# The last output tile of a hybrid decoder's down projection: own buffer for its third weight, an earlier first split, and its second half in two parts of 128 tokens

## The chip, the cores and the metric

The kernel runs on one core of one Trainium2 chip. Its time is the device time of one execution in microseconds (us), and lower is better. TensorE (PE in the profile) multiplies matrices out of SBUF into PSUM, ScalarE (ACT), VectorE (DVE) and GpSimd (POOL) work elementwise, and the queues of SyncE (SP) and POOL issue transfers.

## The reference, cut to what matters

One inference step of a decoder layer for 544 tokens (512 of a prompt, 32 of samples), model width 1024. Everything before the feed-forward network is left out here, since the change does not touch it:

```python
def rmsnorm(x, g):
    x32 = x.astype(jnp.float32)
    y = x32 * lax.rsqrt(jnp.mean(x32 * x32, axis=-1, keepdims=True) + RMS_EPS)
    return (y * g.astype(jnp.float32)).astype(x.dtype)
...
    f = rmsnorm(x, g_ffn_pre)
    g_, u_ = jnp.split(f @ w_gate_up, 2, axis=-1)
    x = x + rmsnorm((jax.nn.silu(g_) * u_) @ w_down, g_ffn_post)
```

`w_down` has 2816 rows (22 blocks of 128) and 1024 columns (8 tiles of 128). The change is in the last of the 8 tiles of `(silu(g) * u) @ w_down` and in the norm, the residual sum and the store that follow it.

## The kernel before, in words

**Products.** The output is made transposed, one tile of 128 output columns at a time: the weight block (128x128) is loaded into TensorE, the tokens stream through it, and the tile stands in PSUM as 128 columns by 544 tokens. To keep precision with the one-pass number format, each factor is split into a rounded high part and the rest: ScalarE writes `w_hi` by a copy (`hi`), VectorE writes `w_lo = w_raw - w_hi` (`lo`), and each block of 128 rows of `w_down` costs three matmuls per piece of tokens: high by high, low by high, high by low. Each of these matmuls loads its own 128x128 weights first, which the profile shows as LDWEIGHTS on a row of its own, PEld.

**Order of the end.** Tile 0 is made plainly, tiles 1 to 6 two at a time by a scheme with fewer products (`block_product`, `plain_rest`, L1571 and L1586), and tile 7, the last, plainly again by `down_steps` (L1533). Its weights come in three chunks of 8, 8 and 6 blocks, c = 0, 1, 2 (`DOWN_K`), in two ring slots: chunk 0 in slot 1, chunk 1 in slot 0, chunk 2 in slot 1 again. So chunk 2 can be transferred to `w_raw[1]` only after chunk 0 was split, and split only after chunk 0's products are done. On the SP queue its transfer also stands behind the 12 transfers of tile 5's `move_y`.

**Halves.** For the last tile the 544 tokens are cut at `LAST_CUT` = 288: half 0 is 256 prompt tokens and the 32 samples, half 1 the other 256 prompt tokens. Token rows are taken two apart, so token tiles `tt` = 0 and 1 are the even and the odd tokens of half 0, `tt` = 2 and 3 those of half 1, and `TT` = 4 are the samples. Chunk 0 is multiplied for both halves, then chunks 1 and 2 for half 0; then, while half 1's chunks 1 and 2 are multiplied, half 0 goes through its chain: ScalarE takes squares and scaled values out of PSUM (`y_half`), TensorE sums the squares over the 1024 columns by matmuls with a column of ones (`sum_part`: of `yacc`, the squares of tiles 0 to 6, and of `ysq`, those of tile 7) and transposes the tile (`half_T`), ScalarE takes the root (`y_roots`) and copies the transposed tile to `ytok` (`half_copy`), VectorE takes the reciprocal and makes `ytok * 1/rms + x1tok` for each token tile in one pass of 1024 columns (L2872), and SP stores it. When half 1's products are done, the same chain runs for half 1 with nothing beside it.

**Moves.** Tiles 0 to 6 reach `ytok` by a 32x32 block transpose on VectorE and 12 small transfers per tile (`move_y`): tiles 0 to 4 on POOL's queue, tiles 5 and 6 on SP's.

Of the kernel before, what the change touches and what calls it, by code (L numbers as in the profile page):

```python
# [130 lines left out]
def program(nc, x_prompt, x_sample, cache_k, cache_v, page_table, state_conv, state_h,  # L131
# [251 lines left out]
    with ExitStack() as ctx:  # L383
# [271 lines left out]
        def _(sp_):  # L655
# [269 lines left out]
        def _(e):  # L925
# [139 lines left out]
            e.dma_start(x1tok[:, 0, :], token_rows(x1_dram, 0)).then_inc(x1_back, 16)  # L1065
            e.dma_start(x1tok[0:TS, TT, :], x1_dram[SEQ:T, :]).then_inc(x1_back, 16)


        @block.tensor
        def _(e):  # L1070
# [545 lines left out]

            def sum_part(sums, tts):

                for tt in tts:
                    rows = TS if tt == TT else P  # L1620
                    mm = e.matmul(y_total(tt)[0:rows], y_cols(sums[:, :], tt), ones[:, 0:1],
                                  start=sums is yacc, stop=sums is ysq, skip_group_check=True)
                return mm

            def half_T(h):

                e.wait_ge(y_free, KD + 2 + h)
                e.wait_ge(yt_free, h + 1)
                for tt in (0, 1) if h == 0 else (2, 3):
                    mm = e.transpose(ps[:, YT_BANK, tt * P:tt * P + P], y_cols(yg[1][:, :], tt), ident[:, :])  # L1630
                if h == 0:
                    mm = e.transpose(ps[0:TS, YT_BANK + 1, 0:P], y_cols(yg[1][:, :], TT), ident[:, :])
                mm.then_inc(yt_ready, 1)
# [27 lines left out]
        def _(e):  # L1661
# [486 lines left out]
            def y_half(h):  # L2148

                m, cols = KD - 1, slice(LAST_CUT, T) if h else slice(0, LAST_CUT)  # L2150
                n = cols.stop - cols.start
# [3 lines left out]
                e.activation(ysq[:, cols], ps[:, D_PAIR_BANK + h, 0:n], ACT.Square).then_inc(y_sq_last, 1)  # L2155
                e.activation(yg[1][:, cols], ps[:, D_PAIR_BANK + h, 0:n], ACT.Identity, scale=prm[:, m + 48:m + 49]
                             ).then_inc(y_free, 1)

            def y_roots(h):

                e.wait_ge(yn_ready, h + 1)
                tts = slice(2 * h, 2 * h + 2)
                sums = ps[:, 2:4, 0] if h else ps[:, 2 * D_PAIR[0], tts]
                last = e.activation(ycol[:, tts], sums, ACT.Sqrt, bias=eps_col[:, :], scale=1.0 / D)
                if h == 0:
                    last = e.activation(ycol[0:TS, TT:TT + 1], y_total(TT)[0:TS], ACT.Sqrt, bias=eps_col[0:TS, :],
                                        scale=1.0 / D)
# [24 lines left out]
            for n in range(N7):  # L2192
# [36 lines left out]
        def _(e):  # L2229
# [605 lines left out]
            for n in range(N7):  # L2835
# [66 lines left out]
```

## Time and profile before

| | us |
|---|---|
| median of 3 runs | 765.9 |
| lowest and highest | 765.15 and 766.57 |
| the profiled execution's own time | 766.97 |
| its span, first to last instruction | 765.2 |

The span leaves out what lies around the first and the last instruction, so it is shorter than the execution's own time by 1.77 us. The profiled execution is 1.07 us slower than the median of the runs. Lines of the profile name the engine, the source line, the operation, and output<-input; a shape such as `128*128 128x256` is the loaded weight block and the streamed operand.

### The profile page before, as it was taken

To read this page: it belongs to the slowest core of one execution; us is meant where nothing else is said; L and a number is where in the kernel's file an instruction comes from. 1 tells how busy PE (TensorE), PEld (TensorE's weight loads), DVE (VectorE), ACT (ScalarE), POOL (GpSimd) and SP (SyncE) were. 2 spreads that over 40 slices of the span, in tenths; PEclk is the share of its full clock that TensorE was granted. 3 is DMA by queue.
4 is the path that set the end of the run, shared out by engine and by line. 5 is a ranking of instruction groups with operands and counts; after the bars stand their busy time and mean duration, and the time that the engine had idled before them with its cause. 6 is when DMAs were issued, how large, how long until landed. Compare 5 with 4: busy or idle time off the path is not lost.

```text
span 765.2 us, 16115 instructions
## 1 busy us (share of the span) xinstructions
PE 753.7 (98%) x5909; PEld 713.0 (93%) x5909; DVE 520.2 (68%) x822; ACT 376.4 (49%) x670; POOL 109.2 (14%) x216
## 2 busy tenths in 40 slices
PE   8999999999999999999999999999999999999995
PEld 6998899898898999987899999999999999999995
DVE  7547747656665575784569887787777899665543
ACT  7334725534733642343466555545545468444432
POOL 6602012020120110013000000000000000363510
PEclk9999999999999999999999999999999999999998
DMA  8645555545543315515561333323333212434283
GB/s 260 168 112 118 156 136 115 149 102 114 148 123 99 90 57 170 165 65 179 169 194 29 111 110 110 96 80 98 110 110 104 60 49 84 136 90 112 63 230 129
DMA packets 187065, 91.77 MB, mean 120 GB/s; under 512 B 54582, under 2 KB 179978, under 8 KB 187020
## 3 DMA queue, kind: packets, MB, share of 16 engines
q1 hardware_dynamic: 181342, 82.97, 39.6%
q0 software_dynamic: 4496, 7.85, 3.4%
q8 instruction: 28, 0.46, 0.3%
q10 hardware_dynamic: 1182, 0.35, 0.2%
q14 instruction: 17, 0.14, 0.1%
HBM read 82.37 MB, written 6.81 MB: 117 GB/s over the span
## 4 chain that ended last, share of the span: by engine, by line
PE 93%; DVE 2%; DMA 2%; SPq 1%; ACT 1%; issue 0%; DVEq 0%
PE ps L1080 34%; PE ps L1469 28%; PE ps L1363 6%; PE ps L1586 6%; PE ps L1571 5%; PE ps L1533 3%; PE ps L1437 3%; PE ps L1187 1%; PE ps L1201 1%; PE ps L1219 1%; DMA w_raw<-in_w_down_dram 1%; DMA w_raw<-in_w_in_dram 1%; SPq L647 1%; PE ps L1261 1%; PE ps L1172 1%; PE ps L1371 1%
## 5 line engine op out<-in xcount | busy, mean ns | idle before, releaser
L1080 PE MATMUL ps<-xin_hi,w_hi 128*128 128x272 f32 x544 | 117.1, 296 | 1.2 <-DVE w_lo L2256 1.2
L1080 PE MATMUL ps<-xin_hi,w_lo 128*128 128x272 f32 x544 | 112.5, 288 | 0.0
L1080 PE MATMUL ps<-xin_lo,w_hi 128*128 128x272 f32 x544 | 112.2, 288 | 0.0
L2249 DVE TENSOR_TENSOR w_lo<-w_raw,w_hi 128x1024 fp32r<-128x1024 f32 (+1 forms) x47 | 56.9, 1210 | 58.8 <-ACT w_hi L1666 58.4
L1080 PEld LDWEIGHTS ps<-xin_hi,w_hi 128*128 128x128 f32 x544 | 84.8, 188 | 9.5 <-issue 7.6
L1080 PEld LDWEIGHTS ps<-xin_lo,w_hi 128*128 128x128 f32 x544 | 85.4, 188 | 0.0
L1080 PEld LDWEIGHTS ps<-xin_hi,w_lo 128*128 128x128 f32 x544 | 85.0, 189 | 0.0
L1666 ACT ACTIVATE w_hi<-w_raw 128x1024 fp32r<-128x1024 f32 (+1 forms) x48 | 50.1, 1045 | 55.6 <-PE ps L1080 45.4
L647 POOL DMA_DIRECT2D ytok<-yz x40 | 28.1, 709 | 307.6 <-DVE yz L2810 307.6
L1469 PE MATMUL ps<-xq_lo,b_hi 128*128 128x272 f32 x160 | 46.6, 292 | 0.0
L1469 PE MATMUL ps<-xq_hi,a_lo 128*128 128x272 f32 x160 | 46.4, 290 | 0.0
L1469 PE MATMUL ps<-xq_lo,a_hi 128*128 128x272 f32 x160 | 46.2, 289 | 0.0
L1469 PE MATMUL ps<-xq_hi,b_hi 128*128 128x272 f32 x160 | 46.2, 288 | 0.0
L1469 PE MATMUL ps<-xq_hi,b_lo 128*128 128x272 f32 x160 | 46.1, 288 | 0.0
L1469 PE MATMUL ps<-xq_hi,c_hi 128*128 128x272 f32 x160 | 46.1, 288 | 0.0
L1469 PE MATMUL ps<-xq_hi,a_hi 128*128 128x272 f32 x160 | 46.1, 288 | 0.0
L1469 PE MATMUL ps<-xq_hi,c_lo 128*128 128x272 f32 x160 | 45.9, 287 | 0.0
L1469 PE MATMUL ps<-xq_lo,c_hi 128*128 128x272 f32 x160 | 45.9, 287 | 0.0
L1988 ACT ACTIVATE a_hi<-g_raw 128x1024 fp32r<-128x1024 f32 x20 | 21.2, 1062 | 20.8 <-PE ps L1469 17.9
L1469 PEld LDWEIGHTS ps<-xq_hi,b_hi 128*128 128x128 f32 x160 | 30.2, 188 | 0.0
L1469 PEld LDWEIGHTS ps<-xq_hi,b_lo 128*128 128x128 f32 x160 | 30.1, 188 | 0.0
L1469 PEld LDWEIGHTS ps<-xq_lo,a_hi 128*128 128x128 f32 x160 | 30.1, 188 | 0.0
(394 smaller groups left out, 2134.7 us busy)
## 6 DMA issues: line engine op xcount, KB each, us to landing
w_raw<-in_w_in_dram SPq DMA_DIRECT2D x68, 256.0 KB, 3.3
g_raw<-in_w_gate_up_dram SPq DMA_DIRECT2D x40, 256.0 KB, 3.8
u_raw<-in_w_gate_up_dram SPq DMA_DIRECT2D x20, 256.0 KB, 3.1
e_raw<-in_w_gate_up_dram SPq DMA_DIRECT2D x20, 256.0 KB, 4.3
raw_p<-in_w_down_dram SPq DMA_DIRECT2D x24, 192.0 KB, 2.6
kc<-in_cache_k_dram SPq DMA_DIRECT2D x64, 64.0 KB
vc<-in_cache_v_dram SPq DMA_DIRECT2D x64, 64.0 KB
raw<-in_w_down_dram SPq DMA_DIRECT2D x12, 320.0 KB, 3.1
```

The source lines that it names most:

```text
L647: e.dma_start(prompt[:, 2 * part:2 * part + 2, d, :], yz[s][rows, c0:c0 + 2 * P]).then_inc(moved, 16)
L1080: mm = e.matmul(ps[:, bank + h, 0:HT], wt[:, kw, :], xt[:, kx, h * HT:h * HT + HT], start=first and wt is wh and xt is xh, stop=last and ( ...
L1172: e.matmul(ps[GR * g:GR * g + GR, S_BANK, 0:PAST], q_bd[:, b, :], kcT[:, b, :], start=b < NG, stop=b >= NG, skip_group_check=True)
L1363: mm = e.matmul(ps[:, o_bank(tt) + c, :], xt[:, k, tt * P:tt * P + P], wt[:, c * NHALF:(c + 1) * NHALF], start=k == K_ORDER[0] and xt is x ...
L1437: mm = e.matmul(ps[:, 4 * m + 2 * c + h, 0:HT], wt[:, k, :], xt[:, x, k % KQ, :], start=k == 0 and wt is wh and xt is xq_hi, stop=k == KD ...
L1469: mm = e.matmul(ps[:, bank, 0:HT], wt[:, k0 + k, :], xt[:, x, k, :], start=first and k == 0 and wt is wh and xt is xq_hi, stop=last and k ...
L1533: mm = e.matmul(ps[:, D_BANK[odd] + h, 0:cols.stop - cols.start], wt[:, k, :], x, start=first and k == ks[0] and wt is wh and not lo_x, st ...
L1571: mm = e.matmul(ps[:, bank, 0:HT], wt[:, k, :], xt, start=first and k == 0 and wt is wh and xt is xh, stop=last and k == SK - 1 and wt is ...
L1586: mm = e.matmul(ps[:, banks[h], 0:HT], wt[:, k, :], x, start=firsts[h] and i == 0 and k == 0 and wt is wh and not lo_x, stop=lasts[h] and ...
L1666: e.activation((to or w_hi[s])[:, 0:k, :], w_raw[s][:, 0:k, :], ACT.Copy).then_inc(hi_done, count)
L1988: e.activation(a_hi[:, :, :], g_raw[s][:, :, :], ACT.Copy).then_inc(a_h, 1)
L2249: e.tensor_tensor(wl[:, 0:k, :], w_raw[s][:, 0:k, :], wh[:, 0:k, :].bitcast(F32), ALU.subtract).then_inc(lo_done, count)
```

## The change

What it does, by engine:

- A buffer `raw_last` for chunk 2's raw weights, in the place of `hs[0]`, which the pair scheme has finished reading by then. SP issues its transfer right after those of chunks 0 and 1, behind a wait on `op_used`, and tile 5's 12 transfers go to the end of POOL's queue.
- ScalarE's split of chunk 0 waits for one piece less of tile 5 and 6's products (`OPS7 * N7 - 2` for `- 1`); VectorE's half of it has the old wait.
- Half 1 is made in two parts of 128 tokens (`last_part`), the even and the odd tokens, each in its own PSUM bank, read from `hid_hi` and `hid_lo` with a stride of two. The end has three stages instead of two: half 0, part 0, part 1.
- VectorE adds half 0's squares of tile 7 to `yacc`, so half 0's sums need one matmul for each token tile instead of two.

The diff, cut to its core:

```diff
+    raw_last = put("raw_last", [P, DOWN_K[2], P], where=[hs_at[0]])
...
-            for part in range(3):
-                move_y(e, KD - 3, 1, part, y_moved_last)
-            load(C_LAST + 2, 1, wd[:, KF - DOWN_K[2]:KF, (KD - 1) * P:KD * P], DOWN_K[2])
+            e.wait_ge(op_used, OP_0 + OPS7 * (N7 - 1) + OP_S1 + 1)
+            e.dma_start(raw_last[:, :, :], wd[:, KF - DOWN_K[2]:KF, (KD - 1) * P:KD * P]).then_inc(raw_in["11"], 16)
...
+            def last_part(c, ks, part, last):
+
+                wh, wl = w_hi[(1 + c) % 2], w_lo[(1 + c) % 2]
+                k0 = sum(DOWN_K[:c])
+                out = ps[:, LAST_BANK[part], 0:P]
+                for k in ks:
+                    for wt, lo_x in ((wh, False), (wh, True), (wl, False)):
+                        x = (hid_lo[:, k0 + k, LAST_CUT:T] if lo_x else hid_hi[k0 + k][:, LAST_CUT:T]
+                             ).rearrange("p (n s) -> p s n", s=2)
+                        mm = e.matmul(out, wt[:, k, :], x[:, part], start=c == 0 and k == 0 and wt is wh and not lo_x,
+                                      stop=last and k == ks[-1] and wt is wl, skip_group_check=True)
+                return mm
...
-            down_steps(0, 1, range(DOWN_K[0]), True, False, cut=LAST_CUT).then_inc(tile_done, 1)
+            down_steps(0, 1, range(DOWN_K[0]), True, False, hs=(0,), cut=LAST_CUT)
+            last_part(0, range(DOWN_K[0]), 0, False)
+            last_part(0, range(DOWN_K[0]), 1, False).then_inc(tile_done, 1)
             for c in (1, 2):
                 split_ready(last + c)
                 mm = down_steps(c, 1, range(DOWN_K[c]), False, c == 2, hs=(0,), cut=LAST_CUT)
             mm.then_inc(tile_done, 1)
-            down_steps(1, 1, range(4), False, False, hs=(1,), cut=LAST_CUT)
-            e.wait_ge(ysq_used, KD)
-            for tt in (0, 1, TT):
-                sum_part(yacc, (tt,))
-                if tt == 0:
-                    e.wait_ge(y_sq_last, 1)
-                mm = sum_part(ysq, (tt,))
-            mm.then_inc(yn_ready, 1)
+            last_part(1, range(6), 0, False)
+            e.wait_ge(ysq_used, KD + 1)
+            sum_part(yacc, (0, 1, TT), True).then_inc(yn_ready, 1)
             half_T(0)
-            down_steps(1, 1, range(4, DOWN_K[1]), False, False, hs=(1,), cut=LAST_CUT)
-            down_steps(2, 1, range(DOWN_K[2]), False, True, hs=(1,), cut=LAST_CUT).then_inc(tile_done, 1)
-            sum_part(yacc, (2, 3))
+            last_part(1, range(6, DOWN_K[1]), 0, False)
+            last_part(2, range(DOWN_K[2]), 0, False).then_inc(tile_done, 1)
+            last_part(1, range(DOWN_K[1]), 1, False)
+            sum_part(yacc, (2,))
             e.wait_ge(y_sq_last, 2)
-            sum_part(ysq, (2, 3)).then_inc(yn_ready, 1)
+            sum_part(ysq, (2,)).then_inc(yn_ready, 1)
             half_T(1)
+            last_part(2, range(DOWN_K[2]), 1, True).then_inc(tile_done, 1)
+            sum_part(yacc, (3,))
+            e.wait_ge(y_sq_last, 3)
+            sum_part(ysq, (3,)).then_inc(yn_ready, 1)
+            half_T(2)
...
-            e.wait_ge(op_used, OP_0 + OPS7 * N7 - 1)
+            e.wait_ge(op_used, OP_0 + OPS7 * N7 - 2)
             hi(C_LAST, C_LAST // 2, 1, DOWN_K[0])
...
+            e.wait_ge(op_used, OP_0 + OPS7 * N7 - 1)
             lo(C_LAST, 1, DOWN_K[0])
```

The first place is the end of SP's queue, from the transfers of chunks 0 and 1 (`w_raw_50`, `w_raw_49`) to tile 6's `move_y`. Before:

```order
L668 DMA w_raw_50<-in_w_down_dram 128x4x128 [waits lo_done,s_done]
L668 DMA w_raw_50<-in_w_down_dram 128x4x128
L668 DMA w_raw_49<-in_w_down_dram 128x4x128 [waits lo_done]
L668 DMA w_raw_49<-in_w_down_dram 128x4x128
L647 DMA ytok<-yz_216 128x2x32 [waits y_turned,consts]
L647 DMA ytok<-yz_216 128x2x32 x7
L649 DMA ytok<-yz_216 32x32 x4
L668 DMA w_raw_50<-in_w_down_dram 128x4x128 [waits lo_done]
L668 DMA w_raw_50<-in_w_down_dram 128x2x128
L647 DMA ytok<-yz_215 128x2x32 [waits y_turned,consts]
L647 DMA ytok<-yz_215 128x2x32 x7
L649 DMA ytok<-yz_215 32x32 x4
```

After:

```order
L670 DMA w_raw_50<-in_w_down_dram 128x4x128 [waits lo_done,s_done]
L670 DMA w_raw_50<-in_w_down_dram 128x4x128
L670 DMA w_raw_49<-in_w_down_dram 128x4x128 [waits lo_done]
L670 DMA w_raw_49<-in_w_down_dram 128x4x128
L909 DMA raw_last<-in_w_down_dram 128x6x128 [waits s_mm]
L649 DMA ytok<-yz_215 128x2x32 [waits y_turned,consts]
L649 DMA ytok<-yz_215 128x2x32 x7
L651 DMA ytok<-yz_215 32x32 x4
```

Chunk 2's transfer now stands ahead of all of `move_y`, and tile 5's 12 transfers (`yz_216`) have left this queue; tile 6's (`yz_215`) stay.

The second place is TensorE where half 0's sums and transposes stand between the products of the other half (`w_hi_51` and `w_lo_53` are chunk 1's split weights, `w_hi_52` and `w_lo_54` chunk 2's). Before:

```order
L1533 MATMUL ps<-hid_hi_203,w_hi_51 128x256 [waits hid_l]
L1533 MATMUL ps<-hid_lo,w_hi_51 128x256
L1533 MATMUL ps<-hid_hi_203,w_lo_53 128x256
L1621 MATMUL ps<-ones,yacc 128x1 [waits ysq_used]
L1621 MATMUL ps<-ones,ysq 128x1 [waits y_sq_last]
L1621 MATMUL ps<-ones,yacc 128x1
L1621 MATMUL ps<-ones,ysq 128x1
L1621 MATMUL ps<-ones,yacc 32x1
L1621 MATMUL ps<-ones,ysq 32x1
L1630 MATMUL ps<-ident,yg_227 128x128 [waits yt_free,y_free]
L1630 MATMUL ps<-ident,yg_227 128x128
L1632 MATMUL ps<-ident,yg_227 32x128
```

After:

```order
L1629 MATMUL ps<-hid_lo,w_hi_51 128x128
L1629 MATMUL ps<-hid_hi_205,w_lo_53 128x128
L1638 MATMUL ps<-ones,yacc 128x1 [waits ysq_used]
L1638 MATMUL ps<-ones,yacc 128x1
L1638 MATMUL ps<-ones,yacc 32x1
L1647 MATMUL ps<-ident,yg_227 128x128 [waits yt_free,y_free]
L1647 MATMUL ps<-ident,yg_227 128x128
L1652 MATMUL ps<-ident,yg_227 32x128
L1629 MATMUL ps<-hid_hi_206,w_hi_51 128x128
```

The three sums of `ysq` are gone, and the products around them are 128 columns wide instead of 256. In the last tile as a whole there were 66 matmuls of 128x256 and there are 132 of 128x128; the 66 of 128x288 are unchanged.

The third place is the end of VectorE's program. Before:

```order
L2249 TENSOR_TENSOR w_lo_54<-w_raw_50,w_hi_52 128x768 [waits hi_done]
L2862 RECIPROCAL ycol<-ycol 128x2 [waits y_root,x1_back]
L2864 RECIPROCAL ycol<-ycol 32x1
L2872 SCALAR_TENSOR_TENSOR ytok<-ytok,ycol,x1tok 128x1024 [waits y_moved,y_moved_last,yt_free,y_inv]
L2872 SCALAR_TENSOR_TENSOR ytok<-ytok,ycol,x1tok 128x1024
L2872 SCALAR_TENSOR_TENSOR ytok<-ytok,ycol,x1tok 32x1024
L2862 RECIPROCAL ycol<-ycol 128x2 [waits y_root]
L2872 SCALAR_TENSOR_TENSOR ytok<-ytok,ycol,x1tok 128x1024 [waits y_moved,y_moved_last,yt_free,y_inv]
L2872 SCALAR_TENSOR_TENSOR ytok<-ytok,ycol,x1tok 128x1024
```

After:

```order
L2885 TENSOR_TENSOR w_lo_54<-raw_last,w_hi_52 128x768 [waits hi_done]
L2890 TENSOR_TENSOR yacc<-yacc,ysq 128x288 [waits ysq_used,y_sq_last]
L2895 RECIPROCAL ycol<-ycol 128x2 [waits y_root,x1_back]
L2897 RECIPROCAL ycol<-ycol 32x1
L2905 SCALAR_TENSOR_TENSOR ytok<-ytok,ycol,x1tok 128x1024 [waits y_moved,y_moved_last,yt_free,y_inv]
L2905 SCALAR_TENSOR_TENSOR ytok<-ytok,ycol,x1tok 128x1024
L2905 SCALAR_TENSOR_TENSOR ytok<-ytok,ycol,x1tok 32x1024
L2895 RECIPROCAL ycol<-ycol 128x1 [waits y_root]
L2905 SCALAR_TENSOR_TENSOR ytok<-ytok,ycol,x1tok 128x1024 [waits y_moved,y_moved_last,yt_free,y_inv]
L2895 RECIPROCAL ycol<-ycol 128x1 [waits y_root]
L2905 SCALAR_TENSOR_TENSOR ytok<-ytok,ycol,x1tok 128x1024 [waits y_moved,y_moved_last,yt_free,y_inv]
```

The addition to `yacc` is new, and the last group of two passes over `ytok` has become two groups of one.

## Rows read from the trace of the kernel before

**Rows 1.** The page, busy time: us, share of the span, instructions.

```profile
PE 753.7 (98%) x5909; PEld 713.0 (93%) x5909; DVE 520.2 (68%) x822; ACT 376.4 (49%) x670; POOL 109.2 (14%) x216
```

**Rows 2.** Windows, 748 to 757 us.

```profile
748.00:757.00 9.00, 8.69 (x72) 8.65 (x73) 2.81 (x5) 2.50 (x8) 0.00 (x0) 1.00 0.16 29
```

**Rows 3.** Timeline of TensorE: start us, us, engine, line, what, count.

```profile
736.71 0.41 PE L1586 MATMUL ps<-hid_hi,op_lo 128*128 128x272 f32 x2
...
737.28 0.52 PE L1533 MATMUL ps<-hid_hi,w_hi 128*128 128x288 f32 x2
...
737.63 0.41 PE L1533 MATMUL ps<-hid_lo,w_hi 128*128 128x288 f32 x2
...
743.40 0.29 PE L1533 MATMUL ps<-hid_hi,w_hi 128*128 128x288 f32 x1
...
746.46 0.29 PE L1533 MATMUL ps<-hid_hi,w_lo 128*128 128x288 f32 x1
...
748.31 0.40 PE L1533 MATMUL ps<-hid_hi,w_hi 128*128 128x288 f32 x1 [1.55 <-DVE w_lo L2249]
...
748.55 0.30 PE L1533 MATMUL ps<-hid_lo,w_hi 128*128 128x288 f32 x1
...
752.22 0.29 PE L1621 MATMUL ps<-ones,yacc 128*128 128x1 f32 x2
...
753.94 0.28 PE L1533 MATMUL ps<-hid_lo,w_hi 128*128 128x256 f32 x1
...
757.24 0.28 PE L1533 MATMUL ps<-hid_hi,w_lo 128*128 128x256 f32 x1
...
757.36 0.52 PE L1621 MATMUL ps<-ones,yacc 128*128 128x1 f32 x4
```

**Rows 4.** Timeline of ScalarE, VectorE, SP and POOL, 714 to 755 us.

```profile
714.40 5.62 POOL L647 DMA_DIRECT2D ytok<-yz  x8 [3.90 <-DVE yz L2810]
...
728.16 3.17 SPq L668 DMA_DIRECT2D w_raw<-in_w_down_dram  x4
...
734.90 1.06 ACT L1666 ACTIVATE w_hi<-w_raw 128x1024 fp32r<-128x1024 f32 x1 [2.57 <-PE ps L1586]
...
736.00 1.23 DVE L2249 TENSOR_TENSOR w_lo<-w_raw,w_hi 128x1024 fp32r<-128x1024 f32 x1 [1.81 <-ACT w_hi L1666]
...
742.58 1.13 SPq L668 DMA_DIRECT2D w_raw<-in_w_down_dram  x2
...
746.42 0.84 ACT L1666 ACTIVATE w_hi<-w_raw 128x768 fp32r<-128x768 f32 x1 [6.20 <-DMA w_raw<-in_w_down_dram]
...
747.29 0.96 DVE L2249 TENSOR_TENSOR w_lo<-w_raw,w_hi 128x768 fp32r<-128x768 f32 x1 [5.69 <-ACT w_hi L1666]
...
754.65 3.67 DVE L2872 SCALAR_TENSOR_TENSOR ytok<-ytok,ycol,x1tok 128x1024 f32<-128x1024 f32 x3 [0.47 <-ACT ytok L2177]
```

**Rows 5.** Timeline of TensorE's weight loads at two places.

```profile
748.31 0.19 PEld L1533 LDWEIGHTS ps<-hid_hi,w_hi 128*128 128x128 f32 x1 [1.79 <-DVE w_lo L2249]
...
748.42 0.19 PEld L1533 LDWEIGHTS ps<-hid_lo,w_hi 128*128 128x128 f32 x1
...
757.24 0.55 PEld L1621 LDWEIGHTS ps<-ones,yacc 128*128 128x128 f32 x4
```

**Rows 6.** Groups of weight loads by form, then one timeline row of TensorE.

```profile
L1533 PEld LDWEIGHTS ps<-hid_hi,w_hi 128*128 128x128 f32 x88 | 14.6, 188 | 2.3 <-DVE w_lo L2249 2.2
...
L1201 PEld LDWEIGHTS ps<-ident,lgt 128*128 128x128 f32 x80 | 9.0, 141 | 2.6 <-issue 2.5
...
7.64 0.38 PE L1125 MATMUL ps<-bktab,rel 128*128 128x128 f32 x2
```

**Rows 7.** Timeline of ScalarE, VectorE and SP after the last product.

```profile
757.56 0.38 ACT L2155 ACTIVATE ysq<-ps 128x256 f32<-128x256 f32 x1 [3.01 <-PE ps L1533]
...
759.46 2.48 DVE L2872 SCALAR_TENSOR_TENSOR ytok<-ytok,ycol,x1tok 128x1024 f32<-128x1024 f32 x2 [0.33 <-ACT ytok L2174]
...
760.77 1.53 SPq L915 DMA_DIRECT2D out_dram<-ytok  x2
```

More of the change, by code:

```diff
@@ L633, in program @@
         D_PAIR_BANK = 2 * D_PAIR[1]
+        LAST_BANK = (2 * D_PAIR[1] + 1, 2 * D_PAIR[0] + 1)
         def move_y(e, m, s, part, moved):
@@ L1066, in _ @@
             e.dma_start(x1tok[0:TS, TT, :], x1_dram[SEQ:T, :]).then_inc(x1_back, 16)
+            for part in range(3):
+                move_y(e, KD - 3, 1, part, y_moved)
         @block.tensor
@@ L1615, in _, with sum_part @@
                 plain_rest(n, OP_P2, (C21_BANK, C22_BANK), (False, False), (True, True))
-            def sum_part(sums, tts):
+            def last_part(c, ks, part, last):
[9 more added lines that the diff above has]
+                return mm
+            def sum_part(sums, tts, whole=False):
                 for tt in tts:
                     rows = TS if tt == TT else P
-                    mm = e.matmul(y_total(tt)[0:rows], y_cols(sums[:, :], tt), ones[:, 0:1],
-                                  start=sums is yacc, stop=sums is ysq, skip_group_check=True)
+                    x = sums[:, LAST_CUT + (tt - 2) * P:LAST_CUT + (tt - 1) * P] if sums is ysq else y_cols(sums[:, :], tt)
+                    mm = e.matmul(y_total(tt)[0:rows], x, ones[:, 0:1],
+                                  start=sums is yacc, stop=sums is ysq or whole, skip_group_check=True)
                 return mm
@@ L1628, in half_T @@
                 e.wait_ge(yt_free, h + 1)
-                for tt in (0, 1) if h == 0 else (2, 3):
+                for tt in (0, 1) if h == 0 else ():
                     mm = e.transpose(ps[:, YT_BANK, tt * P:tt * P + P], y_cols(yg[1][:, :], tt), ident[:, :])
+                if h > 0:
+                    c0 = LAST_CUT + (h - 1) * P
+                    mm = e.transpose(ps[:, YT_BANK, (h + 1) * P:(h + 2) * P], yg[1][:, c0:c0 + P], ident[:, :])
                 if h == 0:
@@ L2148, in y_half @@
             def y_half(h):
-                m, cols = KD - 1, slice(LAST_CUT, T) if h else slice(0, LAST_CUT)
-                n = cols.stop - cols.start
+                m = KD - 1
+                c0, n = (LAST_CUT + (h - 1) * P, P) if h else (0, LAST_CUT)
+                cols = slice(c0, c0 + n)
+                got = ps[:, LAST_BANK[h - 1], 0:P] if h else ps[:, D_PAIR_BANK, 0:n]
                 e.wait_ge(tile_done, C_LAST + 4 + h)
@@ L2154, in y_half @@
                     e.wait_ge(ysq_used, m + 1)
-                e.activation(ysq[:, cols], ps[:, D_PAIR_BANK + h, 0:n], ACT.Square).then_inc(y_sq_last, 1)
-                e.activation(yg[1][:, cols], ps[:, D_PAIR_BANK + h, 0:n], ACT.Identity, scale=prm[:, m + 48:m + 49]
+                e.activation(ysq[:, cols], got, ACT.Square).then_inc(y_sq_last, 1)
+                e.activation(yg[1][:, cols], got, ACT.Identity, scale=prm[:, m + 48:m + 49]
                              ).then_inc(y_free, 1)
@@ L2161, in y_roots @@
                 e.wait_ge(yn_ready, h + 1)
-                tts = slice(2 * h, 2 * h + 2)
-                sums = ps[:, 2:4, 0] if h else ps[:, 2 * D_PAIR[0], tts]
+                tts = slice(h + 1, h + 2) if h else slice(0, 2)
+                sums = y_total(h + 1) if h else ps[:, 2 * D_PAIR[0], tts]
                 last = e.activation(ycol[:, tts], sums, ACT.Sqrt, bias=eps_col[:, :], scale=1.0 / D)
@@ L2170, in half_copy @@
             def half_copy(h):
-                m, tts = KD - 1, slice(2 * h, 2 * h + 2)
+                m, tts = KD - 1, slice(h + 1, h + 2) if h else slice(0, 2)
                 e.wait_ge(yt_ready, h + 1)
                 last = e.activation(ytok[:, tts, m * P:m * P + P],
-                                    ps[:, 4, 2 * h * P:2 * h * P + 2 * P].rearrange("p (tt c) -> p tt c", c=P), ACT.Copy)
+                                    ps[:, 4, tts.start * P:tts.stop * P].rearrange("p (tt c) -> p tt c", c=P), ACT.Copy)
                 if h == 0:
@@ L2219, in _ @@
             y_pair(KD - 2, 0, c_pair[1], 5 * N7)
-            hi(C_LAST + 2, (C_LAST + 2) // 2, 1, DOWN_K[2])
+            e.wait_ge(raw_in["11"], raw_0["11"] + 16 * N7 + 16)
+            e.wait_ge(tile_done, C_LAST + 3)
+            e.activation(w_hi[1][:, 0:DOWN_K[2], :], raw_last[:, :, :], ACT.Copy).then_inc(hi_done, 1)
             e.activation(ycol[:, 15:16], eps_col[:, :], ACT.Sqrt)
-            for h in range(2):
+            for h in range(3):
                 y_half(h)
@@ L2855, in _ @@
             y_square(KD - 2, 0)
-            lo(C_LAST + 2, 1, DOWN_K[2])
+            e.wait_ge(hi_done, C_LAST + 3)
+            e.tensor_tensor(w_lo[1][:, 0:DOWN_K[2], :], raw_last[:, :, :], w_hi[1][:, 0:DOWN_K[2], :].bitcast(F32), ALU.subtract
+                            ).then_inc(lo_done, 1)
+            e.wait_ge(y_sq_last, 1)
+            e.wait_ge(ysq_used, KD)
+            e.tensor_tensor(yacc[:, 0:LAST_CUT], yacc[:, 0:LAST_CUT], ysq[:, 0:LAST_CUT], ALU.add).then_inc(ysq_used, 1)
             e.wait_ge(x1_back, 16 * (TT + 1))
-            for h in range(2):
-                tts = slice(2 * h, 2 * h + 2)
+            for h in range(3):
+                tts = slice(h + 1, h + 2) if h else slice(0, 2)
                 e.wait_ge(y_root, h + 1)
-                last = e.reciprocal(ycol[:, 8 + 2 * h:10 + 2 * h], ycol[:, tts])
+                last = e.reciprocal(ycol[:, 8 + tts.start:8 + tts.stop], ycol[:, tts])
                 if h == 0:
@@ L2867, in _ @@
                 e.wait_ge(yt_free, h + 2)
-                e.wait_ge(y_moved, 192 * (KD - 3))
-                e.wait_ge(y_moved_last, 2 * 192)
-                for tt in (0, 1, TT) if h == 0 else (2, 3):
+                e.wait_ge(y_moved, 192 * (KD - 2))
+                e.wait_ge(y_moved_last, 192)
+                for tt in (0, 1, TT) if h == 0 else (h + 1,):
                     rows = slice(0, P if tt < TT else TS)
```

## The prediction

> **What bounds the kernel now.** The page's busy times come first: TensorE is busy 98% of the span, no other engine more than 68% [rows 1], so only two things can move the time: TensorE's own work, and the places where it waits or where work follows its last product. The granted clock is 1.00, the 2.4 GHz level, in the stretch of the change [rows 2], so the clock is not one of them. Next the timeline of TensorE over the last tile [rows 3], read for the distance from one start to the next, since a matmul's duration of 0.28 to 0.30 overlaps its neighbours. A matmul of 288 columns comes every 0.133 us (743.40 to 746.46 in 23 steps), one of 256 every 0.118 us (753.94 to 757.24 in 28 steps). Two breaks stand out. After 736.71, a pair 0.25 apart should have been followed at 736.96, but the last tile starts at 737.28, and its first pair takes 0.35 instead of 0.25: 0.42 us lost. After 746.46 the next was due at 746.59 and came at 748.31, and its first step is 0.24 instead of 0.13: 1.83 us lost. The timelines of the other engines tell why [rows 4]: for the first, ScalarE's split starts at 734.90, released by TensorE, and VectorE's at 736.00, 1.23 long. For the second, chunk 2's transfer is issued only at 742.58, ScalarE splits it at 746.42 after 6.20 us of waiting for it, and VectorE at 747.29. Last, what follows the last product at 757.24 with nothing beside it [rows 3, 7]: sums, squares and a copy, then two passes of VectorE in 2.48 us from 759.46, and the second store after that.
>
> **The change, term by term.** The sum is made on the profiled execution's span, 765.2, at the slot after the last product, 757.36 [rows 3], and then for what follows it.
>
> *First split, -0.42.* ScalarE's wait is shortened by one piece, 9 pairs at 0.25, so it may start 2.25 us before 734.90, at 732.65. Its data is issued from 728.16 on [rows 4]. Chunk 2 took 3.84 us from its issue at 742.58 to ScalarE's start; the same lag from the second transfer, some 0.5 later than 728.16, gives 732.5. So ScalarE ends its 1.06 by about 734, VectorE, which keeps the old wait, starts at 734.9 and ends at 736.15, ahead of 736.96. The loss goes as a whole. Were the cover gone it would cost those 0.42 again.
>
> *Third weight, -1.83.* Chunk 2's transfer follows chunk 1's at about 731.3 (728.16 + 3.17) and lands, by the same 3.84 us, near 735.2, or a little later behind its neighbours. What is late next is the wait for chunk 0's products, since the split still goes into slot 1. With the widths below, chunk 0 ends at 736.96 + 24 x 0.133 + 48 x 0.112 = 745.5, the split needs the 1.89 us that it took from ScalarE's start to TensorE's (746.42 to 748.31), so it is ready at 747.6, and TensorE gets there at 745.5 + 24 x 0.133 = 748.7. Hidden, with 1.1 us to spare.
>
> *Moved transfers, 0.* Tile 5's 12 transfers leave SP, where they stood between 731.3 and 742.6, for POOL, which takes 5.62 us for 8 such [rows 4] and less for the four small ones. Even if they start 5 us later than on SP they are all issued by 750, and VectorE first reads `ytok` at 754.65 [rows 4]. POOL has nothing behind them. SP's tile 6 waits for VectorE's transpose as before.
>
> *The narrow parts, +7.0.* 66 matmuls of 256 columns, 66 x 0.118 = 7.8 us, become 132 of 128. The trace has no matmul of rounded factors under 256 columns, so this price is bounded. By columns alone it is 0.118 - 128 x 0.47 ns (the slope from 256 to 288) = 0.058 us. But each matmul brings its own weights, and a load has its own price. Two loads of rounded weights that find TensorE idle start 0.11 apart (748.31, 748.42), and four loads for matmuls of a single column, where nothing is to be streamed, take 0.55 us together, 0.118 apart [rows 5]. A load takes 188 ns in a record; the shorter loads of transposes, 141 ns, [rows 6] are another form and don't count here. At 256 columns stream and load are just equal, at 128 the load is longer. I take 0.112: nearer to 0.11, because `w_hi` and `w_lo` are read contiguously while the tiles under the 0.118 are read with the stride, and a little over it for the strided tokens, whose stream at 0.058 could double before it showed. 132 x 0.112 = 14.8, less 7.8.
>
> The row shows loads of 128 columns 0.11 us apart [rows 5]. The Trainium skill, "TensorE: Matmul & The Clock Gate", section "LDWEIGHTS (loading the stationary operand)", puts a load at its columns / 1.2 in ns, 107 for 128, which agrees and by which this term would be 6.3. The same page's section "Back-to-back issue gap" gives 81 ns as the sustained distance at 128 columns, by which it would be 2.9.
>
> *Half 0's sums, -0.5.* Of six instructions (12 records, from 752.22 on) three remain: four records at 0.118 and two short ones less. VectorE's new addition of 288 columns stands beside 18 products and is done before them.
>
> *Part 0's sums and transpose inside the stream, +0.7.* Four records of sums, 0.47, and one transpose with its change of form stand between products now; before, all of half 1's came behind the last.
>
> Sum up to the last product: -0.42 - 1.83 + 7.0 - 0.5 + 0.7 = +4.95, so the slot is at 762.3.
>
> *Behind it, -1.7.* One pass of VectorE instead of two: the second of 2.48 us goes, 1.20 [rows 7]. Two fewer records of sums, 0.24. Squares of 128 columns instead of 256 (0.38), 0.1; the copy, of the same size, 0.13 (both estimates, from a third of such a row's time going with its columns). Part 0's own pass starts near 760.7 and is over before part 1's, near 763.9. The last store follows the last pass by as much as before.
>
> Net 4.95 - 1.7 = **+3.25 us**: span 768.45, own time 770.2. That execution was 1.07 slower than the median, so on the median it is 765.9 + 3.25 = **769.2**.
>
> **The rivals.** What a measurement of this kernel can tell from no change is about 0.2%, 1.5 us.
>
> *The load hides and the columns decide (faster).* If the load of a narrow matmul went on beside the stream of the one before without limiting it, the distance would be 0.058 and the term -0.1 instead of +7.0: 765.9 - 3.9 = 762.0, with all the waits still hidden (chunk 0 would end at 743.0, the split be ready at 745.1, TensorE there at 746.2). It decides from 0.087 downwards, where the sum is zero. For it: loads are drawn as overlapping, and the busy row calls them so. Against it: the single-column matmuls, 0.118 apart with nothing else to wait for [rows 5]. 5%. A distance between, 0.08 to 0.1, gives 765 to 767.6; 3%. The 81 ns of the Trainium skill, "TensorE: Matmul & The Clock Gate", section "Back-to-back issue gap", would lead there, to 765.0, and no row of this trace bears it out.
>
> *Narrow rounded matmuls go at the raw price.* A raw matmul of 128 columns is two records in 0.38 us [rows 6], 0.11 apart, so 0.22 each. 132 of them cost 29, the term is 21 and the time 783. For it: nothing narrower than 256 occurs among the rounded ones, so no row excludes it. Against it: nothing in the rows shows a rounded matmul split in two at any width. 7%.
>
> *The strided read is slower than twice the contiguous one.* Then the distance is 0.125 to 0.15 and each 0.01 costs 1.3 us: 771 to 774. For it, the strided loads are 8 ns longer per record, a small sign; 5%.
>
> *A wait stays.* If chunk 2's split or tile 5's transfers came late, up to 1.83 would not be gained, 769.5 to 771. It changes only the size and is in the likeliest case's range.
>
> **How the numbers follow.** Forecast 80%: its own range is from 0.109 (-0.4) to 0.118 (+0.8) for the distance, 0.4 for the tail and the waits and as much for the median, 768.2 to 771.2. Together with half a us below, the wait that stays, and most of the strided case it gives 767.6 to 773, which leaves out the faster case, the one between and the raw price, 15%, and some edges. Slower by over 0.2%: 80 + 7 + 5 = 92%. Within 0.2%: 3%. Faster: 5%.
>
> **What would show it.** In the timeline after, the matmuls of 128x128 are 0.11 to 0.118 apart, and PEld fills that stretch without gaps; at 0.06 or 0.22 the step on the narrow parts is wrong. The breaks ahead of the last tile and of chunk 2 are gone, chunk 0's mark comes near 745.5, and the transfer of `raw_last` lands before 740. The last product stands near 762, followed by one pass of VectorE. If VectorE's first pass waited for a transfer, the step on moved transfers would be wrong. If the distance is right and the time still falls, a term that I don't see is in the end of the kernel.

## The result, and the profile after

| | before | after |
|---|---|---|
| median (lowest to highest), us | 766.13 (765.15 to 766.57), 6 runs | 769.17 (768.96 to 770.26), 6 runs |
| the profiled execution's own time, us | 766.97 | 768.96 |
| its span, us | 765.2 | 767.1 |

The change makes the kernel slower: the ratio of after to before is 1.0044, with a 95% interval of 1.0031 to 1.0057, which is 2.4 to 4.4 us. 769.2 had been forecast. Of all executions of this document two lie far from the rest, at a granted clock of 0.65 and 0.56 over their span (one of before, 1043.97 us, and one of the experiment that reads half 1 as two strided runs, 1223.14 us), and no ratio uses them.

The page of after, busy times as in [rows 1]: 60 instructions more on TensorE and 6.0 us more of its time.

```profile
PE 759.7 (99%) x5969; PEld 719.8 (94%) x5969; DVE 519.7 (68%) x824; ACT 376.6 (49%) x674; POOL 117.1 (15%) x228
```

The timeline of TensorE after, the places that answer to [rows 3] (start us, us, engine, line, what, count):

```profile
735.15 0.41 PE L1589 MATMUL ps<-hid_hi,op_lo 128*128 128x272 f32 x2
735.40 0.30 PE L1536 MATMUL ps<-hid_hi,w_hi 128*128 128x288 f32 x1
...
744.05 0.29 PE L1629 MATMUL ps<-hid_hi,w_lo 128*128 128x128 f32 x1
744.16 0.31 PE L1536 MATMUL ps<-hid_hi,w_hi 128*128 128x288 f32 x1
...
751.89 0.71 PE L1638 MATMUL ps<-ones,yacc 128*128 128x1 f32 x6
752.53 0.51 PE L1647 MATMUL ps<-ident,yg 128*128 128x128 f32 x2
...
753.07 0.31 PE L1629 MATMUL ps<-hid_lo,w_hi 128*128 128x128 f32 x1
...
758.43 0.32 PE L1629 MATMUL ps<-hid_hi,w_lo 128*128 128x128 f32 x1
758.57 0.31 PE L1638 MATMUL ps<-ones,yacc 128*128 128x1 f32 x2
...
759.03 0.36 PE L1629 MATMUL ps<-hid_hi,w_hi 128*128 128x128 f32 x1
...
761.05 0.32 PE L1629 MATMUL ps<-hid_hi,w_lo 128*128 128x128 f32 x1
```

Both breaks of [rows 3] are gone: the last tile starts at 735.40, 0.25 after the pair ahead of it, and no row up to 751.89 stands more than 0.16 behind its neighbour. The matmuls of 128 columns are 0.1165 apart (753.07 to 758.43 in 46 steps). Weight loads fill the whole last tile, 25.61 of 25.65 us, as the window from its first product to its last shows (stretch, its length, then busy us and instructions of PE, PEld, DVE, ACT and POOL, then the granted clock):

```profile
735.40:761.05 25.65, 25.65 (x214) 25.61 (x212) 10.11 (x14) 8.10 (x19) 6.88 (x11) 1.00 0.50 138
```

The timelines of the other engines after, which answer to [rows 4] and [rows 7]:

```profile
726.61 3.26 SPq L670 DMA_DIRECT2D w_raw<-in_w_down_dram  x4
729.90 0.51 SPq L909 DMA_DIRECT2D raw_last<-in_w_down_dram  x1
...
734.62 5.64 POOL L649 DMA_DIRECT2D ytok<-yz  x8
740.26 2.02 POOL L651 DMA_DIRECT2D ytok<-yz  x4
...
744.44 0.85 ACT L2247 ACTIVATE w_hi<-raw_last 128x768 fp32r<-128x768 f32 x1 [5.79 <-PE ps L1629]
745.32 0.96 DVE L2885 TENSOR_TENSOR w_lo<-raw_last,w_hi 128x768 fp32r<-128x768 f32 x1 [5.28 <-ACT w_hi L2247]
...
753.82 3.67 DVE L2905 SCALAR_TENSOR_TENSOR ytok<-ytok,ycol,x1tok 128x1024 f32<-128x1024 f32 x3 [0.47 <-ACT ytok L2202]
759.67 1.28 DVE L2905 SCALAR_TENSOR_TENSOR ytok<-ytok,ycol,x1tok 128x1024 f32<-128x1024 f32 x1
...
762.73 1.28 DVE L2905 SCALAR_TENSOR_TENSOR ytok<-ytok,ycol,x1tok 128x1024 f32<-128x1024 f32 x1
```

ScalarE's split of chunk 2 is now released by TensorE and no longer by a transfer: `raw_last`, issued at 729.90, landed 4.8 us later, at 734.7. One pass of VectorE, not two, follows the last product.

To compare executions, two lengths serve below. The *stage* runs from the start of the last pair product to the start of the last product of the last tile, the *tail* from there to the end of the span. Each execution reaches the stage at a moment of its own, though the kernels do the same in their first 700 us: this profiled run of before at 736.84, after at 735.28, and of the ten experiments nine at 735.4 to 736.2 and one at 737.3. The difference between before and after stands already at TensorE's 500th matmul, which starts at 67.69 in before and at 66.20 in after. That is why the spans differ by 2.0 us and the two lengths by 3.5. Each ratio compares a kernel with the runs of before that were made beside it, so the medians of the table do not all come from one set of runs.

| kernel | stage, us | tail, us | median, us | ratio to before (interval) |
|---|---|---|---|---|
| before | 20.40 | 7.94 | 766.13 | |
| after | 25.77 | 6.10 | 769.17 | 1.0044 (1.0031 to 1.0057) |
| third weight alone | 18.56 | 7.95 | 764.13 | 0.9971 (0.9959 to 0.9983) |
| earlier split alone | 20.23 | 7.93 | 766.96 | 1.0016 (1.0002 to 1.0030) |
| everything but the narrow parts | 17.61 | 7.95 | 763.33 | 0.9968 (0.9957 to 0.9980) |
| parts read contiguously | 25.12 | 6.06 | 768.67 | 1.0035 (1.0022 to 1.0047) |

### The profile page after: what moved, and what is told of

Same layout as the page of the kernel before. It is cut to its first block, busy times and chain, and to the rows that moved or that the text cites. A ratio compares the mean times of both kernels' runs of the same rounds, so it can differ in the third digit from the quotient of the medians.

```text
span 767.1 us, 16245 instructions
## 1 busy us (share of the span) xinstructions
PE 759.7 (99%) x5969; PEld 719.8 (94%) x5969; DVE 519.7 (68%) x824; ACT 376.6 (49%) x674; POOL 117.1 (15%) x228
## 4 chain that ended last, share of the span: by engine, by line
PE 97%; ACT 1%; DVE 1%; DMA 1%; issue 0%; ACTq 0%; DVEq 0%
PE ps L1083 34%; PE ps L1472 28%; PE ps L1589 7%; PE ps L1366 6%; PE ps L1574 5%; PE ps L1536 3%; PE ps L1440 3%; PE ps L1629 2%; PE ps L1190 1%; PE ps L1204 1%; PE ps L1222 1%; PE ps L1289 1%; PE ps L1264 1%; DMA rel<-in_rel_bias_dram 1%; PE ps L1374 1%; PE ps L1175 1%
## 5 line engine op out<-in xcount | busy, mean ns | idle before, releaser
L649 POOL DMA_DIRECT2D ytok<-yz x48 | 33.8, 711 | 307.4 <-DVE yz L2837 307.4
```

Source lines behind the costliest of these rows:

```text
L649: e.dma_start(prompt[:, 2 * part:2 * part + 2, d, :], yz[s][rows, c0:c0 + 2 * P]).then_inc(moved, 16)
```

## The experiments

### The parts of the change, one at a time

**Third weight alone.** Before, with `raw_last`, its transfer behind those of chunks 0 and 1, and tile 5's transfers on POOL.

```diff
-            load(C_LAST + 2, 1, wd[:, KF - DOWN_K[2]:KF, (KD - 1) * P:KD * P], DOWN_K[2])
+            e.wait_ge(op_used, OP_0 + OPS7 * (N7 - 1) + OP_S1 + 1)
+            e.dma_start(raw_last[:, :, :], wd[:, KF - DOWN_K[2]:KF, (KD - 1) * P:KD * P]).then_inc(raw_in["11"], 16)
```

> The kernel before with the own place for the third weight alone (its transfer early, tile 5's moves on POOL); widths, halves and the first split's wait as before. If the term for the third weight is right, the break of 1.83 us ahead of chunk 2 is gone and the time is 766.1 - 1.8 = 764.3. If the moves on POOL come late for VectorE's first pass, or the transfer collides with others, part of it comes back as a wait: 764.5 to 766. If the wait was not on the path that ended last, 766.1.

Measured: 764.13, ratio 0.9971. The stage is 1.84 us shorter, where the term was 1.83. The break ahead of chunk 2 is gone, the one ahead of the last tile stays, as the timeline of this kernel shows (in it the next pair would be due at 735.58):

```profile
735.33 0.41 PE L1588 MATMUL ps<-hid_hi,op_lo 128*128 128x272 f32 x2
735.89 0.40 PE L1535 MATMUL ps<-hid_hi,w_hi 128*128 128x288 f32 x1
...
746.39 0.30 PE L1535 MATMUL ps<-hid_hi,w_hi 128*128 128x288 f32 x1
746.52 0.30 PE L1535 MATMUL ps<-hid_lo,w_hi 128*128 128x288 f32 x1
```

**Earlier split alone.** Before, with the shorter wait of ScalarE.

```diff
-            e.wait_ge(op_used, OP_0 + OPS7 * N7 - 1)
+            e.wait_ge(op_used, OP_0 + OPS7 * N7 - 2)
             hi(C_LAST, C_LAST // 2, 1, DOWN_K[0])
...
+            e.wait_ge(op_used, OP_0 + OPS7 * N7 - 1)
             lo(C_LAST, 1, DOWN_K[0])
```

> The kernel before with the earlier first split alone. My theory: the 0.42 us between the pair scheme and the last tile goes, 765.7, which timing alone can't tell from 766.1; the timeline must show the last tile 0.25 us behind the last pair. Rival: ScalarE's new wait is replaced by the one for the transfer, and the gap stays above 0.3 us.

Measured: 766.96, ratio 1.0016 (1.0002 to 1.0030). The runs, 765.27 to 770.66, are thus 1.2 us slower than before, where the stage of the profiled one is 0.17 shorter and its tail the same; nothing in the end of the kernel shows this, and its cause is open. The timeline of TensorE has the first pair on time, but the break ahead of chunk 2 is longer, 2.09 from start to start instead of 1.85:

```profile
735.37 0.41 PE L1586 MATMUL ps<-hid_hi,op_lo 128*128 128x272 f32 x2
735.62 0.41 PE L1533 MATMUL ps<-hid_hi,w_hi 128*128 128x288 f32 x2
...
744.69 0.29 PE L1533 MATMUL ps<-hid_hi,w_lo 128*128 128x288 f32 x1
746.78 0.40 PE L1533 MATMUL ps<-hid_hi,w_hi 128*128 128x288 f32 x1 [1.79 <-DVE w_lo L2249]
```

TensorE reaches the wait for chunk 2 sooner, but that chunk's transfer still stands behind tile 5's twelve: it is issued 5.83 us after the start of the stage for 5.74 before, and ScalarE's split starts 9.39 after it for 9.58. So the stage falls by 0.17 of the 0.42. The edit is worth its term only together with the third weight.

**Everything but the narrow parts.** Both of these, VectorE's addition to `yacc`, and half 1 at 256 columns in two stages as before.

```diff
             down_steps(1, 1, range(4), False, False, hs=(1,), cut=LAST_CUT)
+            e.wait_ge(ysq_used, KD + 1)
+            sum_part(yacc, (0, 1, TT), True).then_inc(yn_ready, 1)
             half_T(0)
             down_steps(1, 1, range(4, DOWN_K[1]), False, False, hs=(1,), cut=LAST_CUT)
             down_steps(2, 1, range(DOWN_K[2]), False, True, hs=(1,), cut=LAST_CUT).then_inc(tile_done, 1)
```

> The changed kernel without the parts: own place for the third weight, earlier first split, half 0's squares added on VectorE, but half 1 as matmuls of 256 columns and the end in two stages as before. My sum: -0.42 - 1.83 - 0.5 = -2.75, so 763.4, and against the changed kernel -5.8. Rival (the parts cost less than I say and a wait takes their place): within 1 us of the changed kernel's 769.2. A second rival: the three gains overlap and give 764 to 765.

Measured: 763.33, ratio 0.9968, faster than both kernels. The stage is 2.79 us shorter than before's, where the three terms give 2.75; the 256-wide matmuls are 0.118 apart, as before (749.71 to 753.00 in 28 steps):

```profile
749.71 0.28 PE L1535 MATMUL ps<-hid_lo,w_hi 128*128 128x256 f32 x1
...
753.00 0.28 PE L1535 MATMUL ps<-hid_hi,w_lo 128*128 128x256 f32 x1
```

From here to after only the narrow parts are added: the stage grows by 8.16 and the tail falls by 1.85. So they alone cost 6.3 us by these marks, and (1.0044 - 0.9968) x 766 = 5.8 by the ratios.

### What a narrow matmul costs

**Parts read contiguously.** After, with the first and the last 128 tokens of half 1 as its parts.

```diff
-                        x = (hid_lo[:, k0 + k, LAST_CUT:T] if lo_x else hid_hi[k0 + k][:, LAST_CUT:T]
-                             ).rearrange("p (n s) -> p s n", s=2)
+                        c0 = LAST_CUT + P * part
+                        x = hid_lo[:, k0 + k, c0:c0 + P] if lo_x else hid_hi[k0 + k][:, c0:c0 + P]
```

> The changed kernel with part 0 and part 1 read as the first and the last 128 tokens of the half, without the stride of two; the last 128 output columns of these tokens come out in another order. If the weight load sets the distance, it stays at 0.116 to 0.118 us and the time at 769.2. If the strided read set it, the distance falls to 0.11 (768.3) or, if the columns alone would then decide, to 0.06 (761.5).

Measured: 768.67, stage 25.12, that is 0.65 less than after's. The distance is 0.1117 (753.64 to 757.66 in 36 steps) for 0.1165, and 132 x 0.0048 = 0.63. So the distance fell as it should have if the strided read had set it, but by 4.8 ns and no further, to what the weight loads alone take: the load sets the floor, and the stride adds a little above it. The ratios of the two kernels, 1.0035 and 1.0044, overlap in their intervals; what tells them apart is the trace.

```profile
753.64 0.28 PE L1629 MATMUL ps<-hid_lo,w_hi 128*128 128x128 f32 x1
...
757.66 0.28 PE L1629 MATMUL ps<-hid_lo,w_hi 128*128 128x128 f32 x1
```

**192 columns.** After, each narrow matmul with 192 contiguous columns.

```diff
-                out = ps[:, LAST_BANK[part], 0:P]
+                out = ps[:, LAST_BANK[part], 0:192]
...
+                        c0 = LAST_CUT + 64 * part
+                        x = hid_lo[:, k0 + k, c0:c0 + 192] if lo_x else hid_hi[k0 + k][:, c0:c0 + 192]
```

> The changed kernel with each of the 132 narrow matmuls widened to 192 contiguous columns (the two parts overlap, so the last tile's columns hold other tokens). By the slope of 0.47 ns per column, 192 columns alone would take 0.088 us. Load theory: still below the load's 0.111, so the distance is 0.111 and the time about 768.7. Stream theory (columns and load add up in part): 64 columns more cost up to 0.03 each, distance 0.115 to 0.14, time 769.3 to 772.6.

Measured: 769.38, ratio 1.0045 (1.0029 to 1.0062), stage 25.15. By the time alone this would be the stream theory (769.3 to 772.6), but stage and distance are those of 128 contiguous columns, so the 0.7 us between the two medians do not come from the matmuls. The distance is 0.1117 (753.51 to 757.64 in 37 steps):

```profile
753.51 0.28 PE L1629 MATMUL ps<-hid_hi,w_hi 128*128 128x192 f32 x1
...
757.64 0.28 PE L1629 MATMUL ps<-hid_lo,w_hi 128*128 128x192 f32 x1
```

A distance that does not change with the columns could also be a fixed price of every matmul, whatever it loads. The trace of before settles this: among half 0's sums the samples' matmuls load 32 columns of weights instead of 128, and these loads come 0.03 apart where those of 128 columns come 0.118 apart [rows 5]:

```profile
753.14 0.14 PEld L1621 LDWEIGHTS ps<-ones,yacc 128*32 128x32 f32 x2
753.20 0.14 PEld L1621 LDWEIGHTS ps<-ones,ysq 128*32 128x32 f32 x2
```

Their matmuls, of a single column like the others, start 0.03 to 0.05 apart. So the floor belongs to the 128x128 load.

**64 columns.** After, each narrow matmul with 64 contiguous columns.

```diff
-                out = ps[:, LAST_BANK[part], 0:P]
+                out = ps[:, LAST_BANK[part], 0:64]
...
+                        c0 = LAST_CUT + P * part
+                        x = hid_lo[:, k0 + k, c0:c0 + 64] if lo_x else hid_hi[k0 + k][:, c0:c0 + 64]
```

> The changed kernel with each of the 132 narrow matmuls cut to 64 contiguous columns; it leaves out half of half 1's tokens in the last output tile. Theory that the weight load sets the distance: 0.111 us as with 128 contiguous columns, the stage from the last pair product to the last product stays at 25.1 us, time about 768.7. Theory that the stream sets it, or a share of it: the distance falls towards 0.03 to 0.09, and the time by 132 times the difference, 758 to 766.5.

Measured: 777.09, ratio 1.0149 (1.0131 to 1.0168), which neither theory gave. The distance is what the load theory says, 0.1117 (740.91 to 745.38 in 40 steps), but then it doubles, between two matmuls of one kind with nothing waited for:

```profile
740.91 0.28 PE L1629 MATMUL ps<-hid_hi,w_hi 128*128 128x64 f32 x1
...
745.38 0.31 PE L1629 MATMUL ps<-hid_lo,w_hi 128*128 128x64 f32 x1
745.50 0.40 PE L1629 MATMUL ps<-hid_hi,w_lo 128*128 128x64 f32 x1
745.72 0.40 PE L1629 MATMUL ps<-hid_hi,w_hi 128*128 128x64 f32 x1
...
746.74 0.44 PE L1536 MATMUL ps<-hid_lo,w_hi 128*128 128x288 f32 x1
```

Windows of the same kernel (columns as above):

```profile
738.00:745.00 7.00, 7.00 (x62) 7.00 (x60) 3.02 (x5) 2.72 (x6) 6.33 (x11) 1.00 1.02 265
745.50:748.50 3.00, 3.00 (x15) 3.00 (x15) 0.96 (x1) 1.84 (x2) 0.00 (x0) 0.50 0.42 52
749.00:758.00 9.00, 9.00 (x77) 8.96 (x75) 1.57 (x4) 1.73 (x6) 0.00 (x0) 1.00 0.01 2
759.30:768.00 8.70, 8.70 (x43) 8.70 (x43) 2.90 (x4) 0.83 (x4) 0.00 (x0) 0.50 0.41 154
```

The granted clock falls from 1.00 to 0.50, the 1.2 GHz level, at 745.5, after 4.8 us of nothing but 64-column matmuls, comes back under the 288-wide ones of chunks 1 and 2 by 749, and is down again in the last stretch. At that level the 64-column matmuls are 0.213 apart. TensorE is shown busy all the time in all four stretches. With 128 columns at nearly the same distance it stays at 1.00, in after and in the contiguous version. The Trainium skill, "TensorE: Matmul & The Clock Gate", section "HAM oscillation — how this bites in real kernels", ties such a fall to gaps in which TensorE is idle; the rows above have none, so here the fall goes with the narrow stream alone. What in that stream brings it about is not shown.

**Stride of four.** After, with 64 columns read with a stride of four.

```diff
-                             ).rearrange("p (n s) -> p s n", s=2)
+                             ).rearrange("p (n s) -> p s n", s=4)
```

> The changed kernel with each of the 132 narrow matmuls reading 64 columns with a stride of four, over the same 256 columns as before; half of half 1's tokens are left out in the last output tile. If the 4.8 ns that the stride of two cost belong to each strided column, half the columns bring half of it, 0.1135 to 0.114, time about 768.4. If they belong to the reading of the whole 256 columns' memory, the distance stays at 0.116 or more, time about 769. If a strided read costs nothing once the stream is far shorter than the load, 0.111, time about 768.1.

Measured: 779.48, ratio 1.0169 (1.0151 to 1.0187), the clock again. At full clock the distance is 0.112 (739.44 to 741.67 in 20 steps), no more than with 64 contiguous columns. A strided stream of 64 columns shows nothing beside the load, so what a strided column costs had to be read where the stream is the longer one.

```profile
739.44 0.28 PE L1629 MATMUL ps<-hid_hi,w_lo 128*128 128x64 f32 x1
...
741.67 0.28 PE L1629 MATMUL ps<-hid_lo,w_hi 128*128 128x64 f32 x1
741.78 0.33 PE L1629 MATMUL ps<-hid_hi,w_lo 128*128 128x64 f32 x1
741.93 0.40 PE L1629 MATMUL ps<-hid_hi,w_hi 128*128 128x64 f32 x1
```

### What the stride costs

**256 columns, strided.** Two kernels on top of the version with two wide stages. The first reads half 1 as two strided runs of 128 columns in one matmul, the second as one strided run of 256 columns out of the first 512 tokens.

```diff
+                                x = x.rearrange("p (n s) -> p s n", s=2)
```

```diff
+                                x = (hid_lo[:, k0 + k, 0:512] if lo_x else hid_hi[k0 + k][:, 0:512]
+                                     ).rearrange("p (n s) -> p s n", s=2)[:, 0]
```

> The version of two 256-wide stages with the third weight's own place and the earlier split, in which half 1's 66 matmuls of 256 columns read their tokens with the stride of two, the even ones and then the odd ones (the last output tile's columns hold the tokens in another order). If the stride costs each column 0.0375 ns, as 4.8 ns over 128 would have it: 0.1175 becomes 0.127, the stage 17.6 becomes 18.2, time 763.3 becomes 763.9. If the 4.8 ns fall on each matmul whatever its width: 0.122, +0.3 us. If the stride costs only where the load is the longer one: 0.1175, no change.

> The version of two 256-wide stages, its half 1 reading every second one of the first 512 tokens as one strided run of 256 columns (so the last output tile's columns hold other tokens there). The version that read 256 tokens in two strided runs had a distance of 0.2285 us where the contiguous one has 0.1175. If the stride halves the rate of the stream, this one has 0.2285 too, stage 24.9 from the last pair product to the last product, time about 770.6. If the two runs cost it (each at least about 0.114), one run has 0.1175, stage 17.6, time 763.3.

Measured: 770.65, ratio 1.0054 (1.0034 to 1.0075), stage 24.86 for the first; 770.24, ratio 1.0051 (1.0037 to 1.0065), stage 24.87 for the second. None of the three prices that I had set for the first was near: its distance is 0.229 (756.66 to 760.78 in 18 steps), twice the contiguous one:

```profile
756.66 0.43 PE L1539 MATMUL ps<-hid_hi,w_lo 128*128 128x256 f32 x1
...
760.78 0.43 PE L1539 MATMUL ps<-hid_hi,w_lo 128*128 128x256 f32 x1
```

The second shows that the stride does it, and not the two runs (756.59 to 760.48 in 17 steps of 0.229):

```profile
756.59 0.43 PE L1538 MATMUL ps<-hid_hi,w_hi 128*128 128x256 f32 x1
...
760.48 0.42 PE L1538 MATMUL ps<-hid_hi,w_lo 128*128 128x256 f32 x1
```

**256 columns in two contiguous runs.**

```diff
+                                x = (hid_lo[:, k0 + k, 0:512] if lo_x else hid_hi[k0 + k][:, 0:512]
+                                     ).rearrange("p (s n) -> p s n", s=2)[:, :, 0:P]
```

> The same version, its half 1 reading two contiguous runs of 128 tokens each (0 to 127 and 256 to 383, so the last output tile's columns hold other tokens there) in one matmul of 256 columns. If the stride halves the rate, there is none here: distance 0.1175, stage 17.6, time 763.3. If two runs in one operand cost it, 0.2285, stage 24.9, time 770.6. If both, between.

Measured: 763.17, ratio 0.9958 (0.9943 to 0.9973), stage 17.70: two runs cost nothing that the stage shows, the distance is 0.118 (750.28 to 753.58 in 28 steps).

```profile
750.28 0.28 PE L1540 MATMUL ps<-hid_lo,w_hi 128*128 128x256 f32 x1
...
753.58 0.28 PE L1540 MATMUL ps<-hid_hi,w_lo 128*128 128x256 f32 x1
```

So a stride of two halves the rate of the stream: 0.229 / 256 = 0.89 ns per column for 0.46. A narrow strided matmul streams for 128 x 0.89 = 0.114, just past the load's 0.111 to 0.112. That is where some 3 of the 4.8 ns of the changed kernel come from; the other 2 are not explained. The Trainium skill, "SBUF — State Buffer", section "Specifications (TRN2)", asks for at least two hits in each 16-byte line for full bandwidth, and says that each step to a new line has a penalty, without its size. A stride of two over 4-byte elements has two hits in a line, and here it runs at half the rate (0.229 for 0.118 us): by the first half of that rule it would not, and the measurement decides.

## Why the prediction was right

**First split, -0.42, and third weight, -1.83.** Right, the second to 0.01 when done alone. The first is worth 0.17 by itself and its 0.42 only with the second, a coupling that the sum used (both were in it) but did not say. Chunk 0 ended at 744.16 + 1.56 (this execution is so much earlier) = 745.7 on the forecast's scale, for 745.5; in the times of the run of after, VectorE's split of chunk 2 is over at 746.28, and TensorE came to chunk 2 only after 24 matmuls of half 0, 3.2 us after 744.16, so at 747.4: 1.1 us to spare, as forecast. That working has a gap: 745.5 and the 1.89 us of the split give 747.4 and 1.3 to spare, not 747.6 and 1.1. The 0.2 that it put in without a word is real, since ScalarE starts its split 0.28 after chunk 0's end.

**Moved transfers, 0.** Right: POOL issues the last of them by 742.28, and VectorE's first pass is released by ScalarE's copy.

**The narrow parts, +7.0.** The mechanism was right, the size a little small: from each start to the next, the 132 matmuls take 15.42 us and the 66 of before took 7.85, so the term is +7.57. The step in error is "a little over it for the strided tokens, whose stream at 0.058 could double before it showed". It does double, to 0.114, and that is past the load. The floor was read rightly from [rows 5]: two loads of contiguous weights 0.11 apart gave it, the strided ones of the sums, 0.118 apart, bounded it from above. The trace of after bears this out, where the sums of `ysq` load contiguous columns: they come 0.111 apart, those of `yacc` still 0.118.

**Against the rivals.** That the columns decide is out, since 64, 128 and 192 contiguous columns all have 0.111 to 0.112, and so are a distance between 0.08 and 0.1 and the raw price, 0.22. No wait stayed. The strided read is not slower than twice the contiguous one, but it is all but twice as slow (0.229 for 0.118 at 256 columns), which leaves the distance at 0.1165 and short of that rival's 0.125. The 81 ns of the Trainium skill, "TensorE: Matmul & The Clock Gate", section "Back-to-back issue gap", do not hold for these operands: 112 contiguous.

**Part 0's chain in the stream, +0.7.** It measures 0.60 (758.43 to 759.03) plus 0.16 less the two distances of 0.116 that would be there anyway, 0.53. **Half 0's sums, -0.5,** are right: from the first of them to the transposes behind it is 1.14 us before and 0.64 after.

**The sum.** Up to the last product +5.37 for +4.95, behind it -1.84 for -1.7, net +3.53 for +3.25; the two errors partly cancel. By the medians it is +3.04, by the ratio +3.4. So the mechanism was right, but that 769.17 was measured where 769.2 had been forecast is luck: the interval alone is 2 us wide. The range, 767.6 to 773.0, was set mostly by the bounds on the distance, and only the lower half of it was needed. The terms that it names for its likeliest case add up to 768.0 to 770.8, where the prediction has 768.2 to 771.2.

**What was left out.** That the changed kernel still runs at full clock is not a matter of course. 64 columns at nearly the same distance bring the clock down and cost 8.4 us more than the contiguous 128 (777.09 against 768.67), a danger for a narrower last part that neither the sum nor the rivals had.

## What to carry to other kernels

Where every matmul brings its own 4-byte 128x128 weights, the load sets a floor of 0.112 us, and cutting a 256-column matmul in two about doubles its cost (2 x 0.1165 for 0.118): the three-stage end bought 1.85 us of tail with 8.16 us of stream. Split the last tile's work only for as few blocks as the shorter tail pays for. As an estimate from these rows, a block of three matmuls costs 3 x (2 x 0.1165 - 0.118) = 0.35 more in two parts, against 1.85 - 0.53 = 1.3 gained (the shorter tail less part 0's chain in the stream), so the split pays for under four blocks. It was not run, and there both parts would stand in one PSUM bank, which ScalarE would read while TensorE still writes into it. And look at the edits of one change apart: here three of them gave 2.8 us, and the fourth hid it.

## What the runs showed that I had not expected

- A stride of two over 4-byte tokens halves TensorE's stream (0.229 for 0.118 us at 256 columns), and is nearly hidden at 128 columns by the load (0.1165 for 0.1117).
- The least distance of two matmuls goes with the width of the weights that they load: 0.112 us with 128 columns of weights, whether 64, 128 or 192 tokens stream, and 0.03 with 32 columns of weights and one streamed.
- A dense stream of 64-column matmuls, 0.112 us apart and shown as busy throughout, has its granted clock fall to 0.50; with 128 columns at 0.112 to 0.116 it stays at 1.00.
- An earlier start of a stage can be worth little while a later wait in it is tied to a transfer: 0.42 became 0.17.
